# The order of weight pieces in a mixture-of-experts loop: down pieces among the up pieces, and the next rows turned in halves

## What is computed

```
logits = xt @ w_router + b_router;  top 4 of 32 experts per token, gates = softmax
for each block of up to 128 rows of one expert e:
    gt  = min(xb @ w_gate[e] + b_gate[e], 7)
    up  = clip(xb @ w_up[e] + b_up[e], -7, 7)
    hdn = (up + 1) * gt * sigmoid(1.702 * gt)
    y   = hdn @ w_down[e] + b_down[e]
out[token] += gate * y
```

## Time and profile before

| what | value |
|---|---|
| median of 3 runs | 1375.0 us (1371.61 to 1377.09) |
| the profiled execution | 1371.91 us, span 1370.2 us |
| mean granted clock of TensorE | 0.977 |
| PE busy | 1271.7 us, 93% |
| DVE busy | 1254.3 us, 92% |
| ACT busy | 985.6 us, 72% |
| POOL busy | 261.6 us, 19% |
| DMA | 475.66 MB, mean 347 GB/s |
| chain that ended last | PE 58%, DVE 17%, issue 11%, ACT 5% |

### The profile page before, as it was taken

One profiled execution on the slowest core, in us unless ns is written; L12 is line 12 of the kernel. 1 busy time (PEld: TensorE's weight loads), 2 busy tenths in 40 slices (PEclk: granted clock), 3 DMA queues, 4 the chain that ended last, 5 costly groups with the idle time before them and its releaser, 6 DMA issues.

```text
span 1370.2 us, 17740 instructions
## 1 busy us (share of the span) xinstructions
PE 1271.7 (93%) x5827; PEld 1021.0 (75%) x5827; DVE 1254.3 (92%) x1021; ACT 985.6 (72%) x785; POOL 261.6 (19%) x195
## 2 busy tenths in 40 slices
PE   4999899878999999999999999999999999999984
PEld 3877667766878787777777787878787877777773
DVE  6899955699999999999999999999999999999998
ACT  3241754448797888888888888887979788888761
POOL 2000000102031212121212222130313121212242
PEclk9999879979999999999999999999999999999997
DMA  9942401399999999999999999999999999999973
GB/s 286 374 162 77 161 1 51 139 364 384 370 412 411 404 417 407 415 410 414 412 414 411 410 411 415 412 413 409 418 410 409 409 409 411 410 421 422 396 296 109
DMA packets 84998, 475.66 MB, mean 347 GB/s; under 512 B 10747, under 2 KB 11046, under 8 KB 35814
## 3 DMA queue, kind: packets, MB, share of 16 engines
q1 hardware_dynamic: 73918, 437.33, 79.6%
q0 software_dynamic: 5984, 21.25, 4.4%
q10 hardware_dynamic: 5064, 16.67, 3.3%
HBM read 445.89 MB, written 29.33 MB: 347 GB/s over the span
## 4 chain that ended last, share of the span: by engine, by line
PE 58%; DVE 17%; issue 11%; ACT 5%; SPq 5%; DMA 2%; ACTq 1%; POOL 0%; DVEq 0%; POOLq 0%
PE pair L1925 13%; PE pair L1927 12%; PE pair L1926 12%; DVE w_low L1282 7%; PE pair L1938 4%; PE pair L1939 4%; DVE area_m L1128 3%; SPq L477 2%; ACT w_high L829 2%; PE pair L1912 2%; PE pair L1945 2%; SPq L467 1%; SPq L487 1%; ACT area_m L904 1%; ACT fold_g L910 1%
## 5 line engine op out<-in xcount | busy, mean ns | idle before, releaser
L1282 DVE TENSOR_TENSOR w_low<-w_raw,w_high 128x2048 fp32r<-128x2048 f32 x380 | 857.5, 2290 | 43.4 <-ACT w_high L829 42.3
L829 ACT CAST w_high<-w_raw 128x2048 fp32r<-128x2048 f32 x380 | 717.9, 1913 | 177.0 <-PE pair L1927 132.7
L1938 PE MATMUL pair<-w_high,xS 128*128 128x512 f32 x480 | 192.7, 401 | 16.1 <-DVE w_low L1282 16.0
L1925 PE MATMUL pair<-w_high,xT_high 128*128 128x512 f32 x528 | 207.1, 392 | 0.6 <-DVE w_low L1282 0.6
L1927 PE MATMUL pair<-w_high,xT_low 128*128 128x512 f32 x528 | 205.8, 390 | 0.0
L1926 PE MATMUL pair<-w_low,xT_high 128*128 128x512 f32 x528 | 205.6, 389 | 0.0
L1939 PE MATMUL pair<-w_low,xS 128*128 128x512 f32 x480 | 187.8, 391 | 0.0
L1938 PEld LDWEIGHTS pair<-w_high,xS 128*128 128x128 f32 x480 | 90.4, 188 | 46.8 <-DVE w_low L1282 22.5
L612 POOL CAST sel_gate<-is_expert 128x128 fp32r (+1 forms) x17 | 65.6, 3861 | 271.4 <-PE pair L1939 248.3
L1925 PEld LDWEIGHTS pair<-w_high,xT_high 128*128 128x128 f32 x528 | 99.2, 188 | 21.4 <-issue 0.7
L1927 PEld LDWEIGHTS pair<-w_high,xT_low 128*128 128x128 f32 x528 | 99.1, 188 | 20.7
(11 more groups left out here) (362 smaller groups left out, 1823.7 us busy)
## 6 DMA issues: line engine op xcount, KB each, us to landing
w_raw<-in_w_gate SPq DMA_DIRECT2D x128, 1024.0 KB, 9.3
w_raw<-in_w_up SPq DMA_DIRECT2D x128, 1024.0 KB, 8.6
w_raw<-in_w_down SPq DMA_DIRECT2D x128, 1024.0 KB, 9.7
ring<-in_w_in SPq DMA_DIRECT2D x5, 2048.0 KB, 17.8
y_rows<-area_t SPq DMA_DIRECT2D x1, 8704.0 KB, 36.9
y_rows<-area_m ACTq DMA_DIRECT2D x15, 512.0 KB, 7.8
ring<-in_w_out SPq DMA_DIRECT2D x2, 2048.0 KB, 8.1
y_rows<-area_t SPq DMA_DIRECT2D x1, 3840.0 KB, 12.7
```

Of the source, the lines that this page charges most:

```text
L829: s.copy(w_high[:, i % HIGH_RING, :], w_raw[i][:, :]).then_inc(high_ready, 1)
L1282: v.tensor_tensor(w_low[i][:, :], w_raw[i][:, :], w_high[:, i % HIGH_RING, :].bitcast(F32), ALU.subtract).then_inc(low_ready, 1)
L1925: t.matmul(to[half], tok_high, hi, start=(opens and kk == 0), stop=False)
L1938: t.matmul(to[half], rows, w_high[:, i % HIGH_RING, cols], start=(opens and kk == 0), stop=False)
```

## The change

The 12 slots of a pass get the order gate 0 to 3, up 0 and 1, down 0 and 1, up 2 and 3, down 2 and 3 (`ORDER`). The loads of SP follow it, with the down pieces taken from the expert of one pass before. TensorE's passes are written out again: the next rows are turned behind slot 5; the fold of gate stands between slots 6 and 7 of the even pass, the fold of up at its end; h is turned behind slot 1 of the even and slot 2 of the odd pass. Since up pieces 2 and 3 are still to come when the next rows are turned, the split rows are written in two halves: the first (k below 4) behind slot 7, the second behind slot 10, once slot 9 is used. `xT_high_ready` and `xT_low_ready` count two per block. ScalarE copies for the fold of up behind slot 10. The small block's limit and product move to slots 0 and 1 of the odd pass, the large block's to slot 10 of it, both together with the second half of rows. The last pass keeps the old order (`act_last`, `dve_last`, `gate`, `up`, `down`). Nothing that is computed changes.

```
+ORDER = (0, 1, 2, 3, 4, 5, 8, 9, 6, 7, 10, 11)
+X_FIRST, UP_DONE = 7, 10
@@ sync
-            for i in (5, 6, 7, 8, 9, 11):
+            for i in (5, 6, 7, 11):
                 load(i, 0)
+            def load_for(slot, e, before):
+                part = ORDER[slot]
+                sp.dma_start(w_raw[slot][:, :], piece_src(part, e if part < DOWN else before)).then_inc(raw_piece[slot], 16)
             second = expert_at(1)
+            for i in (8, 9):
+                load_for(i, second, 0)
...
@@ scalar
+            def x_half(b, second, small, up_done=None):
+                act.wait_ge(xg_transposed, b + 1)
+                if second:
+                    act.wait_ge(piece_used, up_done)
+                if small:
+                    ks = slice(KD // 2 * second, KD // 2 * (second + 1))
+                    s.copy(xS[:, ks, 1, :], turned_small()[:, ks, :]).then_inc(xT_high_ready, 1)
+                else:
+                    s.copy(xT_high[:, second, :], turned()[:, second, :]).then_inc(xT_high_ready, 1)
 act_even:
-                    if not last and i == UP + 2:
+                    if i == X_FIRST:
+                        x_half(j + 2, 0, False)
+                    if i == X_FIRST + 1:
                         silu_small(j + 1, 3 * h + 1)
-                    if not last and i == DOWN:
-                        fold_copy(fold_u, pair[1], base + DOWN)
-                        xT_high_part(j + 2)
+                    if i == UP_DONE:
+                        fold_copy(fold_u, pair[1], base + UP_DONE)
+                        x_half(j + 2, 1, False, base + UP_DONE)
 act_odd:
-                    if i == 2:
+                    if i == 3:
                         hS_part(j)
-                    if i == DOWN:
-                        (xS_part if turn_small else xT_high_part)(j + 2)
+                    if i == X_FIRST:
+                        x_half(j + 2, 0, turn_small)
+                    if i == UP_DONE:
+                        x_half(j + 2, 1, turn_small, base + UP_DONE)
@@ vector
+            def dve_odd(j, h, turn_small=True):
+                base = PIECES * j + 8
+                for i in range(PIECES):
+                    low_part((i + AHEAD) % PIECES, base + i + AHEAD)
+                    if i == 0:
+                        limit_up_small(j, 3 * h + 2)
+                    if i == 1:
+                        hidden_small(j)
+                    if i == 3:
+                        hS_low_part(j)
+                    if i == X_FIRST:
+                        x_low_half(j + 2, 0, turn_small)
+                    if i == UP_DONE:
+                        limit_up(j + 1, base + UP_DONE)
+                        hidden(j + 1)
+                        x_low_half(j + 2, 1, turn_small)
+            def dve_even(j):
+                base = PIECES * j + 8
+                for i in range(PIECES):
+                    low_part((i + AHEAD) % PIECES, base + i + AHEAD)
                     if i == 2:
+                        hT_low_part(j)
+                    if i == X_FIRST:
+                        x_low_half(j + 2, 0, False)
+                    if i == UP_DONE:
+                        x_low_half(j + 2, 1, False)
@@ tensor, pe_even
+                free_for_gate(j + 1)
+                add_bias(G_TO, half_gate, bias_gu)
+                for i in range(4):
+                    if i == 0:
+                        pe.wait_ge(xT_low_ready, 2 * (j + 1) + 1)
+                    piece_small(i, base + i, xS, G_TO, i)
+                    if i == 1:
+                        if not (isinstance(j, int) and j == 0):
+                            fold(fold_d, D_TO, 3 * h)
+                        pe.wait_ge(xT_low_ready, 2 * (j + 1) + 2)
+                        transpose_h(j)
+                pe.wait_ge(u_limited, j + 1)
+                add_bias(U_TO, half_up, bias_gu)
+                for i in range(2):
+                    piece_small(4 + i, base + 4 + i, xS, U_TO, i)
                 pe.wait_ge(hT_low_ready, j + 1)
                 transpose_x(j + 2)
+                free_for_down(j)
+                for i in range(2):
+                    piece(6 + i, base + 6 + i, hT_high, hT_low, D_TO, opens=(i == 0), part=i)
+                    if i == 0:
+                        fold(fold_g, G_TO, 3 * h + 1)
+                for i in range(2):
+                    piece_small(8 + i, base + 8 + i, xS, U_TO, 2 + i)
+                for i in range(2):
+                    piece(10 + i, base + 10 + i, hT_high, hT_low, D_TO, part=2 + i)
+                fold(fold_u, U_TO, 3 * h + 2)
@@ pe_odd
+                for i in range(4):
+                    if i % 2 == 0:
+                        pe.wait_ge(xT_low_ready, 2 * (j + 1) + 1 + i // 2)
+                    piece(i, base + i, xT_high, xT_low, G_TO, part=i)
+                    if i == 2:
+                        transpose_h(j)
...
                 transpose_x(j + 2)
+                free_for_down(j)
+                for i in range(2):
+                    piece_small(6 + i, base + 6 + i, hS, D_TO, i, opens=(i == 0))
+                for i in range(2):
+                    piece(8 + i, base + 8 + i, xT_high, xT_low, U_TO, part=2 + i)
+                for i in range(2):
+                    piece_small(10 + i, base + 10 + i, hS, D_TO, 2 + i)
```

More of the change, by code:

```diff
@@ L1959, in _, with gate @@
             G_TO, U_TO, D_TO = ([bank[i][0:CAP, :], bank[i + 1][0:CAP, :]] for i in (0, 2, 4))
-            def gate(b, base, turn=None, high=xT_high, low=xT_low, between=None, fold_down=None, small=False):
+            def gate(b, base, turn=None, high=xT_high, low=xT_low, between=None, fold_down=None):
                 pe.wait_ge(sel_in_ready, b + 1)
@@ L1980, in gate, with up, down @@
                         between()
-            def up(b, base, high=xT_high, low=xT_low, between=None, fold_gate=None, small=False):
+            def up(b, base, high=xT_high, low=xT_low, between=None):
                 if not (isinstance(b, int) and b == 0):
                     pe.wait_ge(u_limited, b)
-                add_bias(U_TO, half_up if small else sel_up, bias_gu)
+                add_bias(U_TO, sel_up, bias_gu)
                 for i in range(4):
-                    if small:
-                        piece_small(UP + i, base + i, xS, U_TO)
-                    else:
-                        piece(UP + i, base + i, high, low, U_TO)
-                    if i == 1 and fold_gate is not None:
-                        fold(fold_g, G_TO, fold_gate)
+                    piece(UP + i, base + i, high, low, U_TO)
                     if i == 1 and between is not None:
                         between()
-            def down(b, base, place=DOWN, to=D_TO, turn=None, unstored=0, high=hT_high, low=hT_low, fold_up=None, small=False):
+            def down(b, base, place=DOWN, to=D_TO, turn=None, unstored=0, high=hT_high, low=hT_low):
                 pe.wait_ge(hT_low_ready, b + 1)
@@ L2003, in down @@
                 for i in range(4):
-                    if small:
-                        piece_small(place + i, base + i, hS, to, opens=(i == 0))
-                    else:
-                        piece(place + i, base + i, high, low, to, opens=(i == 0))
-                    if i == 1 and fold_up is not None:
-                        fold(fold_u, U_TO, fold_up)
+                    piece(place + i, base + i, high, low, to, opens=(i == 0))
                     if i == 1 and turn is not None:
@@ L2015, in pe_even @@
                 base = PIECES * j + 8
-                gate(j + 1, base, turn=j, small=True, fold_down=None if isinstance(j, int) and j == 0 else 3 * h)
-                up(j + 1, base + UP, small=True, fold_gate=3 * h + 1)
+                free_for_gate(j + 1)
[9 more added lines that the diff above has]
+                        transpose_h(j)
```

146 lines of the change are left out of this document (82 added, 64 removed).

## The result

The changed kernel takes 1384.39 us in the median of 5 runs (1379.94 to 1384.45), the kernel before 1374.09 in the median of 5 beside it. The ratio is 1.0056 (95% interval 1.0041 to 1.0070): slower by 0.56%, an interval clear of no change. The forecast was 1374 us with "no change" as the likeliest (chance 0.52) and a chance of 0.18 for slower. The time lies just inside the range given (1350 to 1385) and outside the 1368 to 1381 that the error of the ledger allowed, and the sign does not agree. The five runs stand at two levels, 1380.0 us (two) and 1384.4 (three); the trace is one of the upper level, and what sets the lower one is not shown.

What follows compares the result with a forecast made beforehand. TensorE and VectorE, both nearly full, were taken to bound each pair by waiting on each other; the longer chain gave -0.05 us a pair, -0.7 us over 14 pairs, ends nothing: 1375.0 - 0.7, 1374 us, range 1350 to 1385.

Steps and rivals of the forecast that it cites:

- the ledger: One pair of passes laid out, each step starting when its last input is there; the longest closed chain is the period.
- The period: Time of one pair of passes in the even stretch: 64.92 us after the change against 64.97 before.
- chain B: Closed chain of a pair through VectorE, ScalarE's full queue, the small product and TensorE to slot 9: 64.92 us.
- Fold of gate: Even pass, moved behind the first large piece: its copy gets over 4 us of cover, its 1.0 us wait goes.
- TensorE becomes the bound: Rival for the pairs: all waits go, 34 us less, 1341 us; chance 0.30 for a gain over 0.5%.
- The objection from the DMA: Against all waits going: 62.6 us a pair needs 427 GB/s; the highest stretch's 422 gives 63.3 us and 1351 us.
- The turn waits longer: Rival, turn of h in the odd pass: halves costing what wholes do give 66.1 us a pair, 1390 us; chance 0.12.
- POOL takes the port: Rival: two POOL casts a pair hold up VectorE, 0.5 us between them, 7 us in all, 1382 us; chance 0.04.
- chain A: Closed chain of a pair through VectorE's gapless queue, then TensorE from the turn of h to slot 9: 64.68 us.
- Ends: Passes outside the loop's pairs: earlier loads, pass 0's 1.5 us wait and the last pass's kept order, costed at nothing.
- the clock: Rival: TensorE's granted clock falls once a pair behind a wait, 1.5 us each, 21 us in all, 1395; chance 0.02.
- The signs named in advance: Profile after: right if period near 64.9; wrong if under 64.4 without the turn's wait, over 65.5, or ends moved over 2 us.

Runs made afterwards that it cites:

- limit_ahead_of_split: Changed kernel with product moved forward, pass 29's half first, early one-hots, plus the large limit ahead of slot 10's split: 1355.71 us, ratio 0.9863 to the kernel before.
- rows_later: limit_ahead_of_split with two row additions of the last pass moved behind the last block's limit and product: 1352.25 us, ratio 0.9837 to the kernel before.
- tail_half_first: Changed kernel with VectorE taking the second half of the next rows ahead of limit and product in pass 29 alone: 1380.39 us, ratio 1.0040.
- extra_odd: Changed kernel with one more VectorE operation of 1.14 us ahead of hS_low behind slot 3 of every odd pass: 1384.45 us, ratio 1.0066.
- turn_behind_slot_3: Changed kernel with the turn of h in the odd pass behind slot 3 instead of slot 2: 1363.55 us, ratio 0.9919.

## Why the prediction was right and wrong

**The period: right.** It was 65.11 us against 64.92. The ledger's links, read again in the trace of the kernel after (the end of a slot is the start of the first matmul behind it). VectorE's first, then TensorE's and ScalarE's:

```profile
710.39 2.29 DVE L1325 TENSOR_TENSOR w_low<-w_raw,w_high 128x2048 fp32r<-128x2048 f32 x1 [0.23 <-ACT w_high L841]
...
725.26 11.10 DVE L1325 TENSOR_TENSOR w_low<-w_raw,w_high 128x2048 fp32r<-128x2048 f32 x5
...
744.33 4.50 DVE L1325 TENSOR_TENSOR w_low<-w_raw,w_high 128x2048 fp32r<-128x2048 f32 x2
...
748.85 1.23 DVE L1552 TENSOR_SCALAR area_q<-pair 64x1024 f32<-64x1024 f32 x1
750.11 2.29 DVE L1325 TENSOR_TENSOR w_low<-w_raw,w_high 128x2048 fp32r<-128x2048 f32 x1
752.44 1.22 DVE L1559 SCALAR_TENSOR_TENSOR area_q<-area_t,area_q 64x1024 f32<-64x1024 f32 x1
```

```profile
708.24 0.39 PE L2000 MATMUL pair<-w_high,hS 128*128 128x512 f32 x1
...
727.61 0.50 PE L1987 MATMUL pair<-w_high,hT_high 128*128 128x512 f32 x1 [0.34 <-DVE w_low L1325]
...
753.72 1.16 PE L1974 MATMUL pair<-ident,area_q 128*128 128x128 f32 x8 [0.93 <-DVE area_q L1559]
754.63 0.47 PE L1987 MATMUL pair<-w_high,xT_high 128*128 128x512 f32 x1
...
773.34 0.39 PE L2000 MATMUL pair<-w_high,hS 128*128 128x512 f32 x1
```

```profile
734.26 1.92 ACT L841 CAST w_high<-w_raw 128x2048 fp32r<-128x2048 f32 x1 [1.22 <-PE pair L1989]
```

| link of chain B | forecast | from | measured |
|---|---|---|---|
| end of slot 9 to the split behind it | 2.14 | 708.24 to 710.39 | 2.15 |
| to the split of slot 6 | 14.85 | to 725.26 | 14.87 |
| to its piece | 2.33 | to 727.61 | 2.35 |
| piece, fold, piece, signal | 6.63 | to 734.26 | 6.65 |
| ScalarE's queue to the split of slot 2 | 10.08 | to 744.33 | 10.07 |
| splits, limit, product | 9.38 | to 753.72 | 9.39 |
| TensorE to the end of slot 9 | 19.51 | to 773.34 | 19.62 |
| sum | 64.92 | | 65.10 |

The largest error of a term, 0.11 of the 0.18 us, is the turn of h: 0.80 us was taken from a turn without a wait; behind one it took 0.91 (753.72 to 754.63). The halves of 128x256, which no row had shown, took 0.33 us as assumed (715.00 to 715.33 on VectorE). The place of the new wait was right too, 1.1 us before the turn in the odd pass against 1.0. Of the remaining 65.11 - 62.6 - 1.2 = 1.3 us, forecast as 1.3 in the even pass, only 0.3 has a row among the waits; from start to start it is 0.6 us ahead of slot 6, and the rest is gaps of tenths ahead of small pieces.

**Fold of gate: right.** In the kernel after it has no wait.

**The rival "TensorE becomes the bound": didn't happen,** but only one order of two operations kept it away: with the product first, half of the 2.4 us of waits went (63.90), with the limit ahead as well 1.5 us (63.46). The forecast had laid the chain through that product and named its place, and treated the order of the list as given. The objection from the DMA isn't answered, it is reached: 26.7 MB in 63.46 us are 421 GB/s, the highest stretch of the earlier trace rows has 422, and the prediction's bound from it was 63.3 us. In the two kernels with a period near 63.46 us ScalarE's casts begin to wait for loads (3 times, 1.7 us in all, between 345 and 1250 us of limit_ahead_of_split; 9 times, 6.1 us, in rows_later), and in no other trace. So the DMA did not hold the period at 65.11, but it may hold it near here.

**The turn waits longer, POOL takes the port: neither.** The halves cost little more than half of the whole, and the product met the turn as drawn. (The 66.1 us of that rival is the sum by chain A, 64.68 + 1.35 = 66.03; its time stands.) POOL's longest operation (last section) stood under VectorE's splits, and these weren't slower.

**Ends: wrong, and this is the step that failed.** "The last pass keeps its order" was costed at nothing. The pass does keep its order, but the pass ahead of it doesn't, and its gate has one wait for both halves of the rows. Four things were missed or mis-sized there. One: the second half stands behind limit and product, 3.0 us more of waiting in pass 30, of which tail_half_first takes 2.4 back. Two: the 14 pairs leave pass 29 apart, and in the new order the odd pass carries the long wait (1.1 us) that the old one had in the even pass: 1.2 us. Three: the wait of pass 0 before slot 6 was priced at 1.5 us in place of 1.5; it was 2.65 in place of 1.3, with a half-speed piece behind it, 1.75 us in all in this trace, though 0.2 in the trace of extra_odd, where half speed set in at the turn already, as in both traces of the kernel before. Four, the clock: the rival was priced at the loop's waits alone, "the ledger's longest is 1.0", while the ends have waits of 2.5 to 3.5 us in both kernels, and the half-speed piece in pass 30 costs 1.6 us (1.0 against what the kernel before lost there itself). Together: 3.0 + 1.0 + 1.2 + 1.8 = 7.0 us. 2.0 more came from the loop (forecast -0.7). These 9.0 us of the two traces stand against 10.3 between the medians and 8.7 between the means. The 2.2 us before the first piece and the 1.2 behind the last turn are within what two traces of the kernel before differ by (4.2 and 1.35 us). Shown by an experiment are the wait of pass 30 and the clock behind it (tail_half_first) and the 1.2 us of pass 29 (turn_behind_slot_3), by traces; how much of each is in the medians is not resolved.

**The signs named in advance:** of what would show it wrong, that the first 340 us or the last 100 move by over 2 us was the one that came true, on both sides, though at the front 2.2 of the 3.9 us are scatter; the signs for the loop came out as written, but for idle gaps of 0.1 us in VectorE's full stretch.

## What to carry to other kernels

Lay the period as a closed chain and then ask of each operation on it which ones beside it in the list nobody awaits: here moving one 2.3 us split behind a 1.2 us product gave 1.3%, while in the loop the new order of pieces gave nothing by itself, since the waits had only moved. An engine that is 95% busy has a price per operation that can be all or nothing, by whether it lies in the gapless stretch; here one added operation in each place told it in two experiments. And the peeled passes at the ends of a loop want the same ledger as the loop: where a buffer is now written in two parts, look up every reader that waits for both at once.

## What the runs showed of the hardware

In the expert passes of all twelve traces no wait of TensorE of up to 1.34 us was followed by a fall of its granted clock. Behind longer ones (2.49 to 3.52 us) it fell in 28 of 34 cases: matmuls then started every 0.43 us instead of 0.23 (1.2 instead of 2.4 GHz) for some 3 to 6 us.

| wait of TensorE | traces | us waited | half speed behind it |
|---|---|---|---|
| turn of h in pass 0 | 12 | 2.49 to 2.58 | 7 |
| slot 6 of pass 0, late one-hots in slot 4 | 5 | 2.65 to 3.52 | 5 |
| first gate piece of pass 30 | 6 | 3.30 to 3.32 | 6 |
| last turn of h | 11 | 3.31 to 3.48 | 10 |

The turn of pass 0 and what follows it ran at full speed in just those five traces in which slot 6 was slow; why is open. The one fast last turn is that of the first trace of the kernel before. With the twelve matmuls behind it, the last turn took 3.8 us at full speed and 5.0 to 6.5 otherwise. So a wait of 3.3 us or more at such a place costs its own length and 1.2 to 2.8 us more in nearly every trace; one of 2.5 us does in about half of them, and two traces of one kernel can differ by it.

The timeline of POOL in the kernel after, in the pair above, has one surprise (both rows copy one column of row numbers, the first in the odd, the second in the even pass):

```profile
699.53 0.48 POOL L612 COPY tok_now<-tok_tab 128x1 int32 x1 [2.46 <-PE pair L1967]
...
727.49 8.92 POOL L612 COPY tok_now<-tok_tab 128x1 int32 x1 [2.51 <-PE pair L1967]
```

The copy of 128x1 numbers took 8.92 us (spans of POOL are rough), until VectorE's five splits in a row (725.26 to 736.36) ended; where VectorE had gaps it took 0.48. The five splits took 11.10 us, as in the earlier trace rows. The Trainium skill, page "SBUF — State Buffer", section "SBUF: two separate sides", describes such an exclusive lock against a VectorE operation with two SBUF inputs; the trace agrees in that POOL is shut out and shows it as the only loser. The copy got no turn between two splits either: its 8.92 us span four of them. It cost nothing here: no wait for the gathered rows is among TensorE's waits in that pair.
